# First compression layer of the samples: three products of 256 columns for each pair of neighbouring spans, chunks turned by 64-wide products

## The chip, the cores and the metric

One core of a Trainium2 chip runs the kernel. The metric is the device time of one execution in microseconds, the median of several.

## The reference

Two layers of a hybrid decoder trunk serve a prompt (512 rows) and a sample group (8 sequences of 4 new rows, with 1024 cached rows each) in one step. The case is about one function of it, the compression of keys and of values for sparse attention:

```python
def _compress(k, pos_emb, w1, w2):          # CMP_STRIDE = 16, hidden 256, 4 KV groups, HEAD_DIM 64
    ch = k[:, :n_chunk * 16].reshape(B, n_chunk, 16, N_KV, HEAD_DIM)
    first  = einsum('bcsgd,sdh->bcgh', ch + pos_emb[:16], w1[:16])
    second = einsum('bcsgd,sdh->bcgh', ch + pos_emb[16:], w1[16:])
    hid = silu(first[:, :-1] + second[:, 1:])
    return einsum('bngh,hd->bngd', hid, w2)
```

A span is two neighbouring chunks of 16 rows. Its hidden values are A c(n) + B c(n+1), with A the first half of w1, B the second and c(n) chunk n. A sample has 64 chunks and so 63 spans for each of 4 groups. The position term is the same for all spans and comes in as a bias. Everything else (projections, short convolution, attention, merge) is untouched.

## The kernel before

TensorE multiplies float32 in three passes: each operand is split into a high part (rounded, written by ScalarE, `...H`) and a low part (the rest, by VectorE, `...L`), and high x high, high x low and low x high are added up in PSUM. These products are of a type that the trace counts as one instruction. Plain float32 products show as two.

A layer runs: projections in feature order (line 769), projections in token order (line 940, six blocks, two buffers), compression, attention of the prompt with that of the samples between (64 units), and output projections.

**Compression** is ten units n = 0 to 9: n = 0 prompt keys, 1 to 4 keys of two samples each, 5 prompt values, 6 to 9 values of two samples each. A unit has four steps j, one for a quarter of the 16 rows of a chunk (rows 4q + j; two source rows, t = 0 and 1, stacked over 128 partitions). The orders of work on PE, ScalarE (act) and VectorE (dve) are written out by hand, one list for each engine, and joined by semaphores:

- `chunk_tp(n, j)` (line 967): PE turns the rows of `craw` for the step, 8 transposes of 128x128 into one of three PSUM banks in rotation. It stands in the middle of a step two ahead (`chunks_ahead`).
- `chunks_high` (ScalarE, line 1647) and `chunks_low` (VectorE, line 2128): eight instructions each of 64x256, from PSUM to `chH` and `chL`, which have two buffers (j % 2).
- `first_layer(n, j)`, line 1017: 24 products a step (2 halves of the hidden values x 4 quarters x 3 passes) of 504 columns, that is 2 samples x 63 spans x 4 groups. The quarters give both the A and the B part, since the moving operand starts `quarter` chunk halves later. For prompts (line 1012), H and L of the chunks go together, 264 and 132 columns.
- `hidden_gate` (ScalarE, line 1658, two sigmoids), `hidden` (VectorE, line 2149), `second_layer` (PE, lines 1035 and 1042), `compressed_out` (VectorE). `second_layer(n - 1)` follows step (n, 0).
- `beside` and `before_chunks`: parts of the prompt's compressed attention and key turns, put between the steps.
- Weights: one DMA from SP brings w1 of the keys (2 MB) into `w1_raw` during the token-order projections, one more brings that of the values as soon as the keys' parts are made. `w1_high` and `w1_low` (lines 1615 and 2100) split a quarter of it, 128x1024.
- After unit 9, PE does `scores(0)`, waits for `compressed_out(8)`, does `scores(1)` and then `second_layer(9)`.

Of the kernel before, what the change touches and what calls it, by code (L numbers as in the profile page):

```python
# [14 lines left out]
ds = bass.ds  # L15
# [130 lines left out]
def build(nc, a):  # L146
    ctx = ExitStack()
    with ctx:
# [96 lines left out]
        chH = at("chH", [P, 2, 2, P, GROUPS], W2, F32R)  # L245
        chL = at("chL", [P, 2, 2, P, GROUPS], W1, F32R)
# [3 lines left out]
        w1_raw = home("w1_raw", [P, 16, HID], M0)  # L250
        craw = [home("craw0", [P, 2, HC, KV], F0), at("craw1", [P, 2, HC, KV], H_H)]
        hidT = at("hidT", [P, 2, 504], 67072)
        hsg = at("hsg", [P, 2, 504], 71104)
        w2 = home("w2", [P, 2, 2, HD], M0 + 16384)
        kcp = [at("kcp0", [P, 2, SEQ], 128512), at("kcp1", [P, 2, SEQ], 76160)]
# [4 lines left out]
        cx = at("cx", [P, 2, SEQ], 80256)  # L260
# [79 lines left out]
        pos_ready = sem("pos_ready")  # L340
# [6 lines left out]
        c_sg, c_hid, c_w2, c_out = sem("c_sg"), sem("c_hid", 2), sem("c_w2", 1), sem("c_out", 1)  # L347
# [113 lines left out]
        def hidden_bank(n):  # L461

            return 4 + 2 * ((n + 1) % 2)
# [28 lines left out]
        def _(sp):  # L492
# [55 lines left out]
            def load_pages(l, n):  # L548

                slot, kv = sample_unit(n) % 2, n // 5  # L550
                numbers = page_numbers(n % 5 - 1)
                if n > 2:
                    sp.wait_ge(c_tp, 64 * l + 8 * sample_unit(n) - 8)
# [5 lines left out]
            def load_w1(l, name):  # L559

                sp.dma_start(w1_raw[:], a[name][ds(l, 1)].rearrange("l (k s) d h -> (s d) (l k) h", s=2)).then_inc(w1_in, 16)
# [9 lines left out]
            for l in range(NL):  # L571
# [14 lines left out]
                for i, c0 in enumerate(KV_COLS):  # L586
# [4 lines left out]
                    if i == 4:  # L591
                        sp.wait_ge(m_out, 16 * l + 16)
                        load_w1(l, "cmp_w1_k")
# [19 lines left out]
                sp.wait_ge(w1_lo, 8 * l + 4)  # L613
                load_w1(l, "cmp_w1_v")
# [4 lines left out]
                sp.wait_ge(c_tp, 64 * l + 64)  # L619
                sp.wait_ge(w1_lo, 8 * l + 8)  # L620
# [60 lines left out]
        def _(pool):  # L681
# [10 lines left out]
            for l in range(NL):  # L692
# [33 lines left out]
                pool.drain().then_inc(sa_q, 1)  # L726

# [21 lines left out]
        def _(pe):  # L749
# [80 lines left out]
            for l in range(NL):  # L830
# [123 lines left out]
                def chunk_tp(n, j):  # L954

                    slot = sample_unit(n) % 2
                    if j == 0:
                        pe.wait_ge(c_in[slot], 1024 * l + 256 * (sample_unit(n) // 2 + 1))
                    for s in range(2):
                        e = 8 * sample_unit(n) + 2 * j + s  # L960
                        if e < 3:
                            pe.wait_ge(tm_ev, nth(tm_ev, l * (5 * TM_BLOCKS) + 5 * TM_BLOCKS - 2))
                        else:
                            pe.wait_ge(c_lo, 64 * l + e - 2)
                        for k in range(4):
                            t, g2 = k // 2, k % 2
                            last = nc.tensor.transpose(ps[:, (e + 2) % 3, k * P:(k + 1) * P],  # L967
                                                       craw[slot][:, s, 2 * j + t, g2 * P:(g2 + 1) * P], ident)
                        last.then_inc(c_tp, 1)

                def chunks_ahead(n, j):

                    if n == 0 and j in (0, 3):
                        chunk_tp(1, int(j == 3))
                    elif n == 5 and j == 1:
                        chunk_tp(6, 1)
                    elif not prompt_unit(n) and j < 2:
                        chunk_tp(n, j + 2)
                    elif not prompt_unit(n) and n < 9 and (n, j) != (4, 3):
                        chunk_tp(n + 2 if n == 4 else n + 1, j - 2)  # L980

                def first_layer(n, j):


                    unit = 10 * l + n
                    nseq, nwin = windows(n)
                    if prompt_unit(n):
                        pe.wait_ge(kp_lo, 8 * l + 4 * (n // 5) + j + 1)
                        pe.wait_ge(w1_lo, 8 * l + (4 * (n // 5) + j + 1))
                    else:  # L990
                        pe.wait_ge(c_lo, 64 * l + 8 * sample_unit(n) + 2 * j + 2)
                    if j == 0:
                        pe.wait_ge(c_hid, nth(c_hid, 2 * unit - 2))
# [10 lines left out]
                    for hid in range(2):  # L1004
                        if hid == 1:
                            chunks_ahead(n, j)
                        for quarter in range(4):
                            span = slice(quarter, quarter + 2 * nwin - 1, 2)
                            if prompt_unit(n):
                                both, cols = pc_x[n // 5][j][:, :, span, :], nwin * GROUPS  # L1010
                                for w, x, width in ((w1H, both, 2 * cols), (w1L, both[:, 0], cols)):
                                    last = nc.tensor.matmul(ps[:, hidden_bank(n) + hid, 0:width], w[j][:, quarter, hid * P:(hid + 1) * P], x,
                                                            start=j == 0 and quarter == 0 and w is w1H, stop=j == 3 and quarter == 3 and w is w1L)
                                continue
# [1626 lines left out]
```

## Time and profile before

| what | value |
|---|---|
| median of 3 runs | 2436.61 us (2434.99 to 2437.31) |
| the profiled execution, its own time | 2438.41 us |
| its span | 2436.6 us, granted clock 0.991 on average |
| busy share PE / PE weight load / VectorE / ScalarE / GpSimd | 96 / 84 / 51 / 41 / 9% |
| compression, layer 1 | about 546 to 811 us |
| compression, layer 2 | about 1753 to 2018 us |

In a row of a view, "PE" is a matmul and "PEld" its weight load, L967 is line 967, `ps<-chH,w1H` means that `ps` is written from `chH` (moving) and `w1H` (stationary), `128*64 128x512` is a stationary tile of 128x64 with 512 moving columns. Durations of matmuls overlap, so their cost is read from start to start. In the chain that ended last, a piece's length is already its contribution to the end.

### The profile page before, as it was taken

The page shows a single profiled execution, that of the slowest core. Times are in us where ns is not written, and L with a number is a line of the kernel's source. Part 1 is how long each engine was busy: PE and PEld are TensorE (multiplying, and loading weights), DVE is VectorE, ACT ScalarE, POOL GpSimd, SP SyncE. Part 2 cuts the span into 40 slices and gives each one's busy share as a digit, 9 for nine tenths or more (in the row PEclk, how much of TensorE's full clock was granted, in tenths as well). Part 3 has the DMA queues.
Part 4 walks back from the last instruction along what each step waited for, and adds up shares of the span by engine and source line. Part 5 has one row for each costly group of instructions (what it writes and reads, how often), then busy time and mean ns, then how long its engine had stood idle before and what let it go on. Part 6 is the DMA issues. An engine that isn't in the chain of part 4 may idle for free.

```text
span 2436.6 us, 45477 instructions
## 1 busy us (share of the span) xinstructions
PE 2349.7 (96%) x17919; PEld 2052.9 (84%) x17919; DVE 1231.4 (51%) x2332; ACT 988.7 (41%) x2024; POOL 209.5 (9%) x349
## 2 busy tenths in 40 slices
PE   8999999999999999899989999999999999998998
PEld 8999999997778655589989999999977885555998
DVE  4444232546675566564454432234667655665544
ACT  4232223435564455533333221234446445554332
POOL 0000000000000233310000000000000002333000
PEclk9999999999999999999999999999999999999999
DMA  6343354707632687663234334546086418867530
GB/s 237 121 139 104 87 169 124 162 19 159 89 51 36 109 123 116 126 197 114 95 116 139 121 104 105 161 115 162 9 174 82 55 16 138 120 108 165 165 113 37
DMA packets 293308, 279.09 MB, mean 115 GB/s; under 512 B 92601, under 2 KB 281465, under 8 KB 291816
## 3 DMA queue, kind: packets, MB, share of 16 engines
q1 hardware_dynamic: 288680, 239.34, 45.1%
q0 software_dynamic: 4416, 36.85, 4.1%
q8 instruction: 142, 2.33, 0.4%
q14 instruction: 70, 0.57, 0.1%
HBM read 249.25 MB, written 43.53 MB: 120 GB/s over the span
## 4 chain that ended last, share of the span: by engine, by line
PE 86%; DVE 6%; ACT 3%; DMA 1%; issue 1%; SPq 1%; DVEq 0%; POOL 0%; ACTq 0%
PE ps L769 47%; PE ps L1017 12%; PE ps L940 7%; PE ps L1144 3%; PE ps L1168 3%; PE ps L1127 2%; DVE chL L2128 2%; PE ps L967 2%; PE ps L1266 2%; PE ps L1042 1%; ACT chH L1647 1%; PE ps L1414 1%; PE ps L1274 1%; SPq L567 1%; DMA v_win<-in_state_win 1%
## 5 line engine op out<-in xcount | busy, mean ns | idle before, releaser
L769 PE MATMUL ps<-hH,wH 128*128 128x272 f32 x2016 | 418.2, 289 | 8.5 <-DVE hL L1971 8.5
L403 DVE TENSOR_TENSOR wL<-w_raw,wH 128x2048 fp32r<-128x2048 f32 (+1 forms) x107 | 246.1, 2300 | 346.1 <-ACT wH L394 343.8
L769 PE MATMUL ps<-hH,wL 128*128 128x272 f32 x2016 | 420.1, 290 | 0.0
L769 PE MATMUL ps<-hL,wH 128*128 128x272 f32 x2016 | 416.9, 288 | 0.0
L769 PEld LDWEIGHTS ps<-hH,wH 128*128 128x128 f32 x2016 | 318.4, 189 | 10.3 <-issue 7.5
L769 PEld LDWEIGHTS ps<-hH,wL 128*128 128x128 f32 x2016 | 317.0, 189 | 0.0
L769 PEld LDWEIGHTS ps<-hL,wH 128*128 128x128 f32 x2016 | 316.9, 189 | 0.0
L2128 DVE TENSOR_TENSOR chL<-ps,chH 64x256 fp32r<-64x256 f32 x512 | 216.6, 423 | 152.6 <-ACT chH L1647 144.9
L1647 ACT ACTIVATE chH<-ps 64x256 fp32r<-64x256 f32 x512 | 207.4, 405 | 207.7 <-PE ps L1017 201.1
L394 ACT ACTIVATE wH<-w_raw 128x2048 fp32r<-128x2048 f32 (+1 forms) x107 | 204.9, 1915 | 97.6 <-PE ps L769 77.6
L739 POOL TENSOR_SCALAR pr<-pr,inv,zg 128x512 f32<-128x512 f32 (+3 forms) x256 | 154.0, 612 | 964.0 <-DVE inv L2323 964.0
L1017 PE MATMUL ps<-chH,w1H 128*128 128x504 f32 x512 | 208.9, 408 | 0.4 <-DVE chL L2128 0.4
L1017 PE MATMUL ps<-chH,w1L 128*128 128x504 f32 x512 | 200.4, 391 | 0.0
L1017 PE MATMUL ps<-chL,w1H 128*128 128x504 f32 x512 | 199.7, 390 | 0.0
L940 PE MATMUL ps<-wH,hH 128*128 128x264 f32 (+1 forms) x480 | 137.1, 286 | 0.0
L940 PE MATMUL ps<-wL,hH 128*128 128x264 f32 (+1 forms) x480 | 136.6, 285 | 0.0
L940 PE MATMUL ps<-wH,hL 128*128 128x264 f32 (+1 forms) x480 | 136.2, 284 | 0.0
L1757 ACT ACTIVATE pr<-ps,nmx 128x512 f32<-128x512 f32 (+3 forms) x256 | 132.2, 526 | 6.4 <-DVE nmx L2315 4.8
L2315 DVE TENSOR_REDUCE nmx<-ps 128x2 f32<-128x1024 f32 (+3 forms) x128 | 105.1, 823 | 36.8 <-PE ps L1132 34.7
L1144 PEld LDWEIGHTS ps<-con,pr 128*128 128x128 f32 x640 | 67.7, 141 | 65.5 <-POOL pr L739 47.8
L1168 PE MATMUL ps<-prT,zv 128*64 128x512 f32 (+3 forms) x512 | 97.2, 454 | 22.5 <-DVE prT L2329 19.6
L1017 PEld LDWEIGHTS ps<-chH,w1H 128*128 128x128 f32 x512 | 96.3, 188 | 26.5 <-issue 8.5
(337 smaller groups left out, 3972.9 us busy)
## 6 DMA issues: line engine op xcount, KB each, us to landing
w_raw<-in_w_in SPq DMA_DIRECT2D x59, 1024.0 KB
craw<-in_cache_kv SPq DMA_DIRECT2D x256, 128.0 KB, 5.0
w_raw<-in_w_in SPq DMA_DIRECT2D x64, 256.0 KB
k_sel<-in_cache_kv SPq DMA_DIRECT2D x128, 128.0 KB, 5.3
v_sel<-in_cache_kv SPq DMA_DIRECT2D x128, 128.0 KB, 10.3
out_new_win_sample<-in_state_win POOLq DMA_DIRECT2D x16, 1016.0 KB, 6.4
w_raw<-in_w_out_a SPq DMA_DIRECT2D x8, 1024.0 KB
k_win<-in_state_win SPq DMA_DIRECT2D x16, 512.0 KB, 7.3
```

Source lines behind the costliest of these rows:

```text
L394: act.activation(block_part(wH, b), block_part(w_raw, b), ACT.Copy).then_inc(w_hi, 1)
L403: dve.tensor_tensor(block_part(wL, b), block_part(w_raw, b), block_part(wH, b).bitcast(F32), ALU.subtract).then_inc(w_lo, 1)
L739: last = pool.tensor_scalar(pr[i % 3][:, g, 0:n], pr[i % 3][:, g, 0:n], inv[:, i % 3, g:g + 1], zg[:, u, gate:gate + 1], ALU.mult, ALU.mult)
L769: last = nc.tensor.matmul(ps[:, bank + hf, 0:HALF], st, x[:, k, hf * HALF:(hf + 1) * HALF], start=k == 0 and w is wH and x is xH, stop=k = ...
L940: last = nc.tensor.matmul(ps[0:rows, tt, 0:width], x[:, k, tt * P:tt * P + rows], w[:, n, k, 0:width], start=k == 0 and w is wH and x is h ...
L1017: last = nc.tensor.matmul(ps[:, hidden_bank(n) + hid, 0:nseq * nwin * GROUPS], w[j][:, quarter, hid * P:(hid + 1) * P], x, start=j == 0 an ...
L1144: last = nc.tensor.transpose(ps[:, 4 + g, kt * P:(kt + 1) * P], pr[i % 3][:, g, kt * P:(kt + 1) * P], ident)
L1168: last = nc.tensor.matmul(ps[rows, bank, kt * P:], zv[:, kt, v0:v0 + HD], turned_queries(g, br, kt), start=False, stop=i % 8 == 7)
L1647: last = act.activation(chH[64 * t:64 * t + 64, j % 2, s, :, g:GROUPS:2], src, ACT.Copy)
L1757: last = act.activation(pr[i % 3][:, g, 0:n], ps[:, 2 * (i % 2) + g, 0:n], ACT.Exp, bias=nmx[:, i % 3, g:g + 1], accum_out=sums[:, i % 3, ...
L2128: last = dve.tensor_tensor(chL[to], src, chH[to].bitcast(F32), ALU.subtract)
L2315: dve.tensor_reduce(out=nmx[:, i % 3, :], in_=ps[:, b:b + 2, 0:P * (unit(i)[2] + 1)], op=ALU.max, axis=AX.X, negate=True).then_inc(pa_nm, 1)
```

## The change

For two neighbouring spans the sums are formed from three products. With chunks 2k and 2k+1: P = A c(2k+1), Q = B c(2k), R = (A + B)(c(2k) + c(2k+1)). Then span 2k is R - P - Q, and span 2k+1 is P(k) + Q(k+1). Each has 256 columns (2 samples x 32 pairs x 4 groups).

- `first_layer`: 24 products of 256 columns (P and Q), then `chunk_tp` for a step two ahead, then 12 products of 256 columns (R) into a bank of its own (`joint_bank`).
- `chunk_tp`: 16 plain float32 products of a 64-wide stationary slice of `craw` with the identity, in pairs for the two halves of the output partitions, instead of 8 transposes. Both samples of a step land in banks 0 and 1, which have no second buffer: it waits for `chunks_low` of the step before.
- Splitting: `odd_chunks` (ScalarE, 128x512), `chunk_sum` (VectorE, 128x512), `chunks_high` (ScalarE, one of 128x1024), `chunks_low` (VectorE, one of 128x1024), `joint_high` (ScalarE, 128x512), `joint_low` (VectorE, 128x512).
- After a unit: `second_part` (ScalarE, 128x512), `hidden_sums` (VectorE, three dependent instructions of 496, 512 and 512 columns with drains), then gate and `hidden` as before. `second_layer(n - 1)` follows step (n, 1).
- Weights: `w1_sum` (VectorE), `w1_joint_high` (ScalarE) and `w1_joint_low` (VectorE), 128x512 each, eight of each in a layer. The joint keys' weights lie in `w1_raw` itself, so the values' weights come in four DMAs of 512 KB from GpSimd's queue, each after step (4, j) and after the DMA before it.
- `hidT` holds the spans of two samples interleaved, so the stationary operand of the values' second layer has a step of 8 elements, not 4.
- VectorE's `beside(4, 0)` and `beside(5, 1)`, with the multiplication of `cs` that stood at (6, 1), move behind `joint_low(7, 0)`, ahead of `chunk_sum(7, 1)`.

```diff
@@ chunk_tp
+                    if e:
+                        pe.wait_ge(c_lo, 96 * l + 3 * e - 1)
                     for s in range(2):
-                        for k in range(4):
-                            last = nc.tensor.transpose(ps[:, (e + 2) % 3, k * P:(k + 1) * P],
-                                                       craw[slot][:, s, 2 * j + t, g2 * P:(g2 + 1) * P], ident)
+                        for g in range(GROUPS):
+                            for t in range(2):
+                                last = nc.tensor.matmul(ps[HD * t:HD * t + HD, s, g * P:(g + 1) * P],
+                                                        craw[slot][:, s, 2 * j + t, g * HD:(g + 1) * HD], ident, start=True, stop=True)
+                    last.then_inc(c_tp, 1)
@@ first_layer, samples
+                    pe.wait_ge(c_lo, t + 2)
                     for hid in range(2):
+                        for odd in (1, 0):
+                            for q in range(2):
+                                ...
+                                for k, (w, x) in enumerate(((wH1, xH), (wH1, xL), (wL1, xH))):
+                                    nc.tensor.matmul(ps[:, bank, (0 if odd else 256):(256 if odd else 512)], w, x, ...)
+                    ...
+                        chunk_tp(n, j + 2)
+                    pe.wait_ge(c_lo, t + 3)
+                    for hid in range(2):
+                        for q in range(2):
+                            for k, (w, x) in enumerate(((SH, xH), (SH, xL), (SL, xH))):
+                                last = nc.tensor.matmul(ps[:, joint_bank(n), 256 * hid:256 * hid + 256], w[:, q, cols], x, ...)
+                    last.then_inc(c_mm, 1)
@@ act
+                def odd_chunks(n, j):
+                    act.wait_ge(c_tp, 32 * l + e + 1)
+                    act.wait_ge(c_lo, 96 * l + 3 * e)
+                    act.activation(ch_sum[:], turned_chunks(slice(2, 4)), ACT.Copy).then_inc(c_hi, 1)
@@ pool
+                for j in range(4):
+                    if l + j:
+                        pool.wait_ge(w1v_in, 64 * l + 16 * j)
+                    pool.wait_ge(c_mm, nth(c_mm, 40 * l + 17 + j))
+                    pool.dma_start(w1_raw[:, j:16:4, :], w1v[:, j:16:4, :]).then_inc(w1v_in, 16)
@@ dve, a unit boundary
+                    chunks_low(n, 1)
+                    hidden_sums(n - 1)
+                    joint_low(n, 1)
+                    chunk_sum(n, 2)
+                    hidden(n - 1)
+                    chunks_low(n, 2)
+                    joint_low(n, 2)
+                    chunk_parts(n, 3)
+                    compressed_out(n - 1)
+                    beside(n, 1)
```

## Rows read from the trace of the kernel before

**Rows 1.** The page, part 4: the chain that ended last, by line.
```profile
PE ps L769 47%; PE ps L1017 12%; PE ps L940 7%; PE ps L1144 3%; PE ps L1168 3%; PE ps L1127 2%; DVE chL L2128 2%; PE ps L967 2%; PE ps L1266 2%; PE ps L1042 1%; ACT chH L1647 1%; PE ps L1414 1%; PE ps L1274 1%; SPq L567 1%; DMA v_win<-in_st
```

**Rows 2.** Windows: stretch, width, busy time (x instructions), granted clock, DMA share, GB/s.
```profile
622.60:651.70 29.10, 28.12 (x133) 21.68 (x133) 18.33 (x40) 17.45 (x36) 0.00 (x0) 1.00 0.71 93
661.00:689.00 28.00, 24.80 (x147) 20.75 (x146) 24.01 (x50) 22.80 (x51) 0.00 (x0) 1.00 0.57 76
```

**Rows 3.** Chain that ended last, 540 to 740 us: start, us, what.
```profile
625.33 1.83 PE ps L1035 x4
627.17 2.94 PE ps L1017 x12
630.11 0.87 PE ps L967 x8
630.98 2.76 PE ps L1017 x12
...
637.89 2.76 PE ps L1017 x12
```

**Rows 4.** Timeline of PE, 43 rows of L940 in sequence, first and last.
```profile
535.82 0.29 PE L940 MATMUL ps<-wH,hH 128*128 128x264 f32 x1
...
540.96 0.29 PE L940 MATMUL ps<-wH,hH 128*128 128x264 f32 x1
```

**Rows 5.** Timeline of PE at 820 and at 870 us: start, duration.
```profile
820.40 0.44 PE L1168 MATMUL ps<-prT,zv 128*64 128x128 f32 x4
820.77 0.44 PE L1144 MATMUL ps<-con,pr 128*128 128x128 f32 x2
...
870.18 1.08 PE L1168 MATMUL ps<-prT,zv 128*64 128x512 f32 x4
871.19 1.09 PE L1144 MATMUL ps<-con,pr 128*128 128x128 f32 x8
```

**Rows 6.** Groups by form, whole span: busy us, mean ns | idle before.
```profile
L1647 ACT ACTIVATE chH<-ps 64x256 fp32r<-64x256 f32 x512 | 207.4, 405 | 207.7 <-PE ps L1017 201.1 <-PE ps L967 0.5
...
L1795 ACT ACTIVATE skT<-ps 128x512 f32<-128x512 f32 x64 | 37.2, 600 | 50.0 <-PE ps L1274 33.4 <-PE ps L1266 15.9
...
L1042 PEld LDWEIGHTS ps<-w,hidT 128*63 128x63 f32 x256 | 30.5, 212 | 2.6 <-DVE hidT L2149 2.6
...
L1168 PEld LDWEIGHTS ps<-prT,zv 128*64 128x64 f32 x512 | 27.5, 134 | 50.7 <-issue 27.2 <-ACT prT L1765 17.4
...
L2149 DVE SCALAR_TENSOR_TENSOR hidT<-ps,hb,hsg 128x504 f32<-128x504 f32 x32 | 22.3, 738 | 14.2 <-ACT hsg L1658 13.8
...
L2100 DVE TENSOR_TENSOR w1L<-w_raw,w1H 128x1024 fp32r<-128x1024 f32 x16 | 19.4, 1221 | 17.6 <-ACT w1H L1615 17.6
...
L1615 ACT ACTIVATE w1H<-w_raw 128x1024 fp32r<-128x1024 f32 x16 | 16.6, 1047 | 0.3
...
L2436 DVE TENSOR_TENSOR ssel<-ps,small 128x512 f32<-128x512 f32 x16 | 11.0, 686 | 16.2 <-PE ps L1274 16.2
```

**Rows 7.** Groups by form, 550 to 745 us.
```profile
L2234 DVE TENSOR_REDUCE cmx<-cs 128x64 f32<-128x2048 f32 x1 | 2.3, 2285 | 0.1
```

**Rows 8.** What PE waited for: us in total, times, longest.
```profile
PE ps L967 <- DVE chL L2128: 5.9, 18, 0.3
PE ps L1035 <- DVE hidT L2149: 5.4, 2, 2.7
```

**Rows 9.** Timeline of DVE, 528 to 596 us.
```profile
548.05 1.22 DVE L2100 TENSOR_TENSOR w1L<-w_raw,w1H 128x1024 fp32r<-128x1024 f32 x1 [7.64 <-ACT w1H L1615]
```

**Rows 10.** DMA issues: KB each, median us to landing.
```profile
pin<-in_p_prompt POOLq DMA_DIRECT2D x2, 512.0 KB, 4.2
```

**Rows 11.** Chain that ended last, 735 to 830 us.
```profile
795.52 13.79 PE ps L1017 x60
809.34 0.69 ACT hsg L1658
...
811.57 3.95 PE ps L1042 x32
```

More of the change, by code:

```diff
@@ L1004, in first_layer @@
                     for hid in range(2):
[L1005 to L1014, printed above, removed]
-                            xH, xL = (t[:, j % 2, :, span, :] for t in (chH, chL))
-                            for w, x, first, last_pass in ((w1H, xH, True, False), (w1H, xL, False, False), (w1L, xH, False, True)):
-                                last = nc.tensor.matmul(ps[:, hidden_bank(n) + hid, 0:nseq * nwin * GROUPS],
-                                                        w[j][:, quarter, hid * P:(hid + 1) * P], x,
-                                                        start=j == 0 and quarter == 0 and first, stop=j == 3 and quarter == 3 and last_pass)
@@ new lines, in first_layer @@
+                    SH, SL = w1_joint(n // 5, j)
+                    for hid in range(2):
+                        cols = slice(hid * P, hid * P + P)
+                        for q in range(2):
+                            xH, xL = chS[j % 2][:, 0, q], chS[j % 2][:, 1, q]
+                            for k, (w, x) in enumerate(((SH, xH), (SH, xL), (SL, xH))):
+                                last = nc.tensor.matmul(ps[:, joint_bank(n), 256 * hid:256 * hid + 256], w[:, q, cols], x,
+                                                        start=j + q + k + hid == 0, stop=j == 3 and q == 1 and k == 2 and hid == 1)
@@ new lines, in joint_low, with chunk_parts @@
+                def joint_low(n, j):
+                    e = place(n, j)
+                    dve.wait_ge(c_hi, 96 * l + 3 * e + 3)
+                    high, low = (chS[j % 2][:, k].rearrange("p q (k a) -> p q k a", k=32) for k in range(2))
+                    dve.tensor_tensor(low, ch_sum[:], high.bitcast(F32), ALU.subtract).then_inc(c_lo, 1)
+                def chunk_parts(n, j):
+                    chunk_sum(n, j)
+                    chunks_low(n, j)
+                    joint_low(n, j)
@@ L2280, in _ @@
                 w1_low(1, 0)
+                prompts_low(5, 1)
+                chunk_parts(6, 0)
                 w1_low(1, 1)
[L2282 to L2283 removed]
+                prompts_low(5, 2)
+                prompts_low(5, 3)
                 w1_low(1, 2)
+                hidden_sums(4)
+                w1_low(1, 3)
                 hidden(4)
[L2286 to L2288 removed]
+                chunk_sum(6, 1)
@@ L2289, in _ @@
                 chunks_low(6, 1)
-                compressed_out(4)
-                beside(5, 1)
-                hidden(5)
-                for n in (6, 7, 8):
+                hidden_sums(5)
+                joint_low(6, 1)
+                hidden(5)
+                w1_sum(1, 0)
+                w1_joint_low(1, 0)
+                compressed_out(4)
+                w1_sum(1, 1)
+                w1_sum(1, 2)
+                w1_joint_low(1, 1)
+                w1_sum(1, 3)
+                chunk_sum(6, 2)
@@ new lines, in _ @@
+                w1_joint_low(1, 2)
+                w1_joint_low(1, 3)
+                compressed_out(5)
+                chunks_low(6, 2)
+                joint_low(6, 2)
+                chunk_parts(6, 3)
+                beside(6, 1)
+                chunk_sum(7, 0)
+                before_chunks(6)
+                chunks_low(7, 0)
+                joint_low(7, 0)
+                beside(4, 0)
+                beside(5, 1)
+                chunk_sum(7, 1)
+                for n in (7, 8, 9):
+                    chunks_low(n, 1)
+                    hidden_sums(n - 1)
+                    joint_low(n, 1)
+                    chunk_sum(n, 2)
+                    hidden(n - 1)
@@ L2305, in _ @@
+                hidden_sums(9)
                 hidden(9)
```

425 lines of the change are left out of this document (279 added, 146 removed).

## The prediction

> **What bounds the kernel now.** I read the chain that ended last first: it is TensorE (PE) nearly throughout, and the line of the changed products, L1017, holds 12% of the span, the turning of chunks, L967, 2%, `chunks_low` 2% [rows 1]. So PE's time in the compression counts one to one. The windows show the same inside: in a stretch of the key units PE is busy 28.1 of 29.1 us, VectorE 18.3, ScalarE 17.5, at full clock. Only where the values start (661 to 689) does VectorE, with 24.0 of 28.0 us, hold PE up [rows 2]. In the chain of a unit the reader sees what a step costs: 2.76 (12 products) + 0.87 (8 transposes) + 2.76 = 6.39 us [rows 3]. The waits on PE say how often it lost time: 18 times `chunk_tp` waited for `chunks_low`, and twice the second layer for `hidden` [rows 8]. Where that happened a step took 637.89 - 630.98 = 6.91 us, 0.52 more than 6.39 [rows 3].
>
> **Products.** From start to start a product of 504 columns takes 13.79 / 60 = 0.2298 us [rows 11], one of 264 columns (540.96 - 535.82) / 42 = 0.1224 [rows 4]. The slope is 0.447 ns a column, so 256 columns cost 0.1188. A step has 24 x 0.2298 = 5.52 us before and 36 x 0.1188 = 4.28 after: 1.24 less, 64 steps (2 layers x 8 units x 4): **-79.3 us**. Bounds for one of 256: 0.1146, if the slope alone counts, and 0.1224, that of 264; I take the line through both.
>
> The Trainium skill, "TensorE: Matmul & The Clock Gate" (Back-to-back issue gap), gives N/2.4 + 2.5 ns, 109 ns for 256 columns; by it the sum would be 22 us lower. By that rule 264 columns would take 112.5 ns, and the trace has 122.4, so it does not agree.
>
> **Turning the chunks.** Before: 0.87 us [rows 3]. After: 8 pairs of plain float32 products, 64 wide, 128 columns. Exactly such pairs stand in the attention: with 512 columns a pair takes 871.19 - 870.18 = 1.01 us, with 128 columns 820.77 - 820.40 = 0.37 [rows 5]. The slope is 1.67 ns a column for both products together, 0.213 us a pair; what is left of 0.37, 0.157, is paid once on coming in. On going out, the first 12 products after such a block take 2.94, not 2.76: 0.18 [rows 3]. So 8 x 0.213 + 0.157 + 0.18 = 2.04 us, 1.17 more than before: **+74.9 us**. Bounds: 1.71, if neither end is paid, and from the weight loads. 32 loads and products of the values' second layer take 3.95 us, 0.123 each, paced by loads of 212 ns; the loads here take 134 [rows 6, 11]. Less the difference of 78 ns that is 0.045 an instruction, 1.45 us a block, no bound; in proportion it is 0.078, 2.49 us. I take the slope, since it is of the same form.
>
> The big gain of the products is thus given back by the turning, nearly to the last microsecond; the rest are waits.
>
> **Round trip of the turned chunks.** The two banks have no second buffer, so `chunk_tp` two ahead waits until `chunks_low` one ahead is done. From the end of one block to the start of the next PE has R (12 x 0.119 = 1.43), 0.18, P and Q (2.85): 4.46 us. In that time must run: end of PE to ScalarE 0.20 (a product lasts 0.17 beyond its slot [rows 4], then 809.31 to 809.34 [rows 11]), `odd_chunks` 0.60, `chunk_sum` 0.69, `chunks_high` 1.05, `chunks_low` 1.22 [rows 6], hand-overs about 0.2: 3.98. Slack 0.48 in a plain step, so the 18 waits of before go: 18 x 0.52 = **-9.4 us**. The 512-byte step of these reads I price at nothing, since L1647 reads so already at 405 ns for 256 columns [rows 6]; on the line between 600 for 512 and 1047 for 1024 that is within 30 ns. ScalarE and VectorE are relieved in total (8 x 0.41 against 2.25 us a step, 8 x 0.42 against 2.6), which is worth nothing by itself off the path.
>
> At a unit's boundary it does not fit. From the end of `chunks_low(n, 1)` there stand in a row: `hidden_sums` 3 x 0.69 + 0.2, `joint_low` 0.69, `odd_chunks` 0.60, two gates 1.38 [rows 11], `chunks_high` 1.05, `chunks_low` 1.22, hand-overs 0.25: 7.46. Counted from the start of unit n, `chunks_low(n, 1)` ends at 3.98 - 1.61 = 2.37, so `chunks_low(n, 2)` ends at 9.83. PE arrives for it after 2.85 + 1.86 + 0.18 + 1.43 + 2.85 = 9.17: wait 0.66, in units 2, 3, 4, 7, 8, 9 of both layers: **+7.9 us**.
>
> **Start of the keys.** `w1_sum` of the first two quarters lies in VectorE's idle 7.64 us [rows 9]; without it each would add 0.69. The others do not hide. Behind `chunks_low(1, 1)` VectorE has `hidden(0)` 0.6, `joint_low` 0.69, four weight instructions 2.76 (with 0.8 waiting for ScalarE's), `compressed_out(0)` 0.5 (the small ones are estimates, scaled down from 0.69 for 512 columns [rows 6]), and then 0.69 + 1.05 + 1.22 for the chunks of (1, 2): 8.3, that is 12.3 after the end of `chunk_tp(1, 1)`. PE gets there after 0.18 + 2.85 + 1.43 + 1.86 + 0.58 + 2.85 = 9.8: wait 2.5, and 0.3 ahead of unit 1. **+5.6 us** in two layers.
>
> **Start of the values.** The last quarter of w1 leaves only after step (4, 3): landing about 4.2 us (512 KB on this queue [rows 10]), 1.05, 1.22, with `hidden_sums(4)` of 2.3 in the way: 9.4 us after unit 4, where PE is ready after 7.8: wait 1.6 (0 to 2.8). From there VectorE has 11 instructions of 512 columns (7.6), two of 1024 (2.4), two hidden layers and two outputs (6.9), 17.5 with waits, before `chunks_low(6, 2)`; PE has 14.4 of work up to `chunk_tp(6, 3)`: wait 3.1 (0 to 4.9). Before, PE lost 2.7 + 0.5 here [rows 8]. **+3.0 us**. Then `beside(4, 0)` and `(5, 1)` stand ahead of `chunk_sum(7, 1)`: two instructions over 2048 columns at 2.29 [rows 7] and seven small ones, 1.5 by estimate, 6.1 us. `chunk_sum(7, 1)` ends 12.1 us after `chunk_tp(7, 0)`, `chunks_low(7, 1)` at 14.5, PE comes at 11.65: wait 2.8, **+5.6 us**. In the old places they hid beside PE's work.
>
> **The end.** Behind unit 9 nothing hides but two `scores`. Before: 811.57 - 809.31 = 2.26 us to `second_layer(9)` [rows 11]. After: 0.20 + 0.60 + 2.27 + 0.69 + 0.74 + 0.74 + 0.1 = 5.34. The attention's first gate and maxima stand behind it: **+6.2 us**.
>
> **Second layer of the values.** The stationary operand's step grows from 16 to 32 bytes. A load of 63 columns with step 16 takes 212 ns, one of 64 without a step 134 [rows 6], so a step costs. If it grows with the distance, eight blocks of 3.95 us double, +31 us; if it is only for leaving the neighbour, nothing. I take nothing, as nearer to a fixed price for each jump.
> The Trainium skill, "SBUF — State Buffer" (the note on cachelines), has lines of 16 bytes and a penalty for each new line; by that both steps pay alike, the sum is the same, and no run here has shown the step of 32 yet.
>
> **Sum.** -79.3 + 74.9 - 9.4 + 7.9 + 5.6 + 3.0 + 5.6 + 6.2 = +14.5 us, on the profiled execution's 2438.4, which stands 1.8 above the median. On the median: **2451 us**. About 5 us (0.2%) can be told from no change.
>
> **Rivals.**
> - *The narrow blocks cost no entry or exit* (the faster side). 64 x 0.34 = 21.7 less, 2429. It decides once a block costs under 2.04 - 14.5 / 64 = 1.81 us. For it: loads can run ahead inside a block. Against: both ends are in the rows [rows 3, 5]. 0.17.
> - *The products run at the slope alone*, 0.1146: 2304 x 0.0042 = 9.7 less, 2441. The row at 264 speaks against it. 0.06. By the gap rule of "TensorE: Matmul & The Clock Gate" in the Trainium skill it would be 22 less, 2429.
> - *Weight loads pace the narrow products.* Midway between 1.71 and 2.49, 0.39 x 64 = 25 more, 2476. 0.12.
> - *Round trip longer than PE's window*: strided reads or hand-overs 25% dearer make it 4.9, 0.4 of wait in some 50 steps, 2471. 0.12.
> - *Second layer of the values doubles*: 2482. 0.05.
> - *The two 64-wide products do not run side by side*: 1.71 x 64 = 109 more, 2560. The slope over 384 columns speaks against it. 0.03.
> - *The waits at starts and boundaries are half of mine* (the DMA lands early, queues overlap better): 28 becomes 14, 2437, no change that can be told. 0.12.
> - *The forecast*, 2443 to 2460: 0.33.
>
> Faster: 0.17 and half of the second, 0.20. Same: 0.15, the halved waits and the rest of the second. Slower: 0.65. The range has to reach 2430 below and 2477 above; the forecast's own is 2443 to 2460.
>
> **What would show it.** Right: 36 starts of L1017's successor at 0.119 us; `chunk_tp` from its first product to R's first in 2.0 us; PE waiting for `chunks_low` about 0.7 us once a unit, and 2 to 3 us in (1, 1), (6, 1) and (7, 0); 5.3 us from unit 9 to its second layer. Wrong: a block under 1.8 or over 2.3 us, a wait in every step, values' loads above 212 ns, or products away from 0.119.

## The result, and the profile after

The changed kernel takes **2459.9 us** (median of 4 runs, 2455.3 to 2463.1) against 2436.0 (2435.0 to 2437.3) for the kernel before in the same session: ratio 1.0096, 95% interval [1.0079, 1.0114], 24 us slower. The forecast was slower, 2451, with a range of 2430 to 2477. So the sign held, the size was 9 us short, and the parts came out less well than the total, as the part on the prediction shows. The profiled execution took 2463.1 us around a span of 2461.3, that is 24.7 above the span of the one before.

The page, part 1 (busy time, share, instructions), part 4 (the chain by line) and part 5 (costliest groups) of the changed kernel:

```profile
PE 2352.6 (96%) x20223; PEld 2109.5 (86%) x20223; DVE 1221.2 (50%) x2068; ACT 934.5 (38%) x1740; POOL 215.6 (9%) x357
...
PE 81%; DVE 8%; ACT 4%; DMA 3%; SPq 2%; issue 2%; DVEq 1%; POOL 0%; ACTq 0%; POOLq 0%
PE ps L812 46%; PE ps L983 7%; PE ps L1009 4%; PE ps L1064 4%; PE ps L1083 3%; PE ps L1232 2%; PE ps L1208 2%; PE ps L1191 2%; PE ps L1329 2%; DVE chL L2280 2%; PE ps L1106 1%; SPq L605 1%; ACT chH L1722 1%; DMA w_raw<-in_cmp_w_v 1%; PE ps 
...
L1009 PE MATMUL ps<-con,craw 128*64 128x128 f32 x2048 | 130.2, 282 | 17.4 <-DVE chL L2280 16.4
```

The 12% of the chain that the changed products held [rows 1] are now 4% (L1064, the products of even and of odd chunks) and 3% (L1083, those of the added ones). The turning of chunks (L1009) has gone from 2% to 4%, and a DMA of first-layer weights, which was not in that list before, has 1%.

What PE waited for (us in total, times, longest), against [rows 8]:

```profile
PE ps L1009 <- DVE chL L2280: 16.4, 10, 2.6
PE ps L1030 <- DVE w1L L2240: 10.3, 6, 2.6
...
PE ps L1106 <- DVE hidT L2321: 5.8, 2, 2.9
```

The 18 short waits of before (at most 0.3 us) are gone, as forecast. In their place stand 10 waits for the turned chunks, eight of them 1.5 to 2.6 us long, and 6 for weights of the values (L1030 are the prompt's products, which need them first).

The chain that ended last, in a plain step of the keys, against [rows 3]:

```profile
611.85 1.61 PE ps L1083 x12
613.46 0.87 PE ps L1123 x8
614.33 2.86 PE ps L1064 x24
617.20 1.90 PE ps L1009 x32
```

24 products in 2.86 us are 0.119 each, to the digit of the forecast. The block of 16 narrow products (x32, as each float32 product is two instructions) takes 1.90, and the 12 products behind it 1.61, where 12 without a block ahead take 1.39 (below, at the end): coming out of the block costs 0.22. A step is 2.86 + 1.90 + 1.61 = 6.37 us against 6.39. **The arithmetic that the change saves is worth next to nothing on this engine's path (0.02 us a step, about 1 us in 64); the 24 us are waits and what follows from them.**

To see where, I took the start of each unit's first product in both traces and subtracted. Sums over both layers; the forecast's terms are laid onto the same stretches (two of a unit's four chunk blocks run ahead of its first product, so unit 1 has two more and unit 9 two fewer than four):

| stretch | forecast, us | measured, us |
|---|---|---|
| up to the start of unit 2 | +8.6 | +4.6 |
| units 2 and 3 | -0.8 | -3.8 |
| start of unit 4 to start of unit 6 (the values' weights) | -2.6 | **+10.6** |
| unit 6 | +3.5 | +6.9 |
| unit 7 | +5.2 | +6.9 |
| unit 8 | -0.4 | -2.1 |
| unit 9, and up to its second layer | +1.1 | +0.1 |
| sum | +14.6 | +23.1 |

The remaining 1.6 of 24.7 us lies outside. One stretch is off by 13 us, the start of the values. The chain there, in the second layer:

```profile
1889.17 9.53 DMA w_raw<-in_cmp_w_v
...
1898.98 4.22 DMA w_raw<-in_cmp_w_v
...
1903.23 1.07 ACT w1H L1681
...
1904.32 1.24 DVE w1L L2240
...
1905.69 3.71 PE ps L1030 x16
1909.39 3.57 PE ps L1102 x4
```

The last quarter of the weights lands in 4.22 us, exactly the price taken from [rows 10], but the quarter ahead of it takes over 9.53, and GpSimd issues one only when the other has landed. In the first layer its timeline reads:

```profile
672.65 0.75 POOL L769 DMA_DIRECT2D w_raw<-in_cmp_w_v  x1 [8.43 <-PE ps L1083]
683.40 0.75 POOL L769 DMA_DIRECT2D w_raw<-in_cmp_w_v  x1 [10.01 <-DMA w_raw<-in_cmp_w_v]
```

Between the issues of the third and the last quarter 10.7 us pass. In that time SyncE's 16 page loads of unit 7, issued between 661.43 and 674.15, are on their way too. So the last step of unit 5 begins 13.7 us after unit 4 instead of 9.4.

The last two lines of the chain above show a second thing: four products of L1102 take 3.57 us, and 1.83 in a key unit. Windows of that stretch (busy times, then granted clock, DMA share, GB/s):

```profile
1899.00:1903.00 4.00, 2.31 (x20) 2.18 (x19) 3.29 (x6) 1.26 (x2) 0.73 (x1) 0.98 0.47 131
1903.00:1913.00 10.00, 7.75 (x24) 4.65 (x23) 4.51 (x6) 3.77 (x5) 0.00 (x0) 0.50 0.00 0
1913.00:1917.00 4.00, 4.00 (x42) 3.87 (x44) 2.55 (x7) 2.20 (x5) 0.00 (x0) 0.99 0.00 0
```

PE had stood idle for 1.69 us up to 1901.18 and for 2.25 up to 1905.69, and from 1903 to 1913 its clock was granted at 0.50, which is 1.2 instead of 2.4 GHz. The same follows three of the four waits for turned chunks of over 1.8 us. Timeline and windows of unit (7, 0), first layer, and two rows of unit 6, the first from the first layer, the second from the same place in the second:

```profile
726.98 2.29 DVE L2419 TENSOR_TENSOR cs<-cs,cgw 128x2048 f32<-128x2048 f32 x1
729.18 0.68 DVE L2274 TENSOR_TENSOR ch_sum<-ps,ch_sum 128x512 f32<-128x512 f32 x1
...
731.02 1.22 DVE L2280 TENSOR_TENSOR chL<-ps,chH 128x1024 fp32r<-128x1024 f32 x1 [1.15 <-ACT chH L1722]
...
732.30 3.52 PE L1009 MATMUL ps<-con,craw 128*64 128x128 f32 x32 [2.61 <-DVE chL L2280]
...
708.84 1.97 PE L1009 MATMUL ps<-con,craw 128*64 128x128 f32 x32 [1.86 <-DVE chL L2280]
1926.23 3.21 PE L1009 MATMUL ps<-con,craw 128*64 128x128 f32 x32 [1.86 <-DVE chL L2280]
```

```profile
729.00:732.00 3.00, 0.69 (x6) 0.49 (x5) 1.85 (x3) 2.03 (x3) 0.00 (x0) 1.00 0.00 0
732.00:735.00 3.00, 2.70 (x26) 2.71 (x28) 2.73 (x5) 0.00 (x0) 0.00 (x0) 0.52 0.00 0
735.00:738.00 3.00, 3.00 (x29) 2.83 (x26) 1.66 (x4) 2.13 (x4) 0.00 (x0) 0.91 0.00 0
```

The queue is the forecast one: `beside(4, 0)` and `(5, 1)` stand ahead of `chunk_sum(7, 1)` (L2274), and PE waits 2.61 us (forecast 2.8). But the block then takes 3.52 instead of 1.97, at a clock of 0.52: wait and slow block cost 4.2 us. The two rows of unit 6 separate the one from the other: behind the same wait of 1.86 us the clock fell in the second layer and stayed in the first, and unit 6 takes 32.8 us there and 31.2 here. So this low clock cost 1.6 us beside the wait, and a wait of this length doesn't always bring it. Over the two compression stretches:

```profile
540.00:840.00 300.00, 280.32 (x2783) 253.08 (x2781) 171.94 (x264) 124.33 (x215) 9.07 (x13) 0.98 0.50 80
1750.00:2060.00 310.00, 291.70 (x2844) 262.92 (x2842) 178.53 (x275) 130.84 (x237) 9.84 (x14) 0.97 0.51 78
```

300 x 0.02 + 310 x 0.03 = 15.3 us of full clock are missing; added up in pieces of 5 us it is the same 15.3, and in the kernel before 1.8. Not all of it is lost time: behind the last wait of each layer, 2.9 us ahead of unit 9's second layer, the clock is low too, and the 32 products there take 4.05 us (below) where they took 3.95 [rows 11]. These two stretches hold 3.4 of the 15.3. Of the other 12 some 10 are lost, by an estimate that takes 1.6 us for each of the four single stretches and the 1.7 us each by which L1102 and the L1030 products ahead of it are slow in the one at 1903. No term of the forecast held this. The Trainium skill, "TensorE: Matmul & The Clock Gate" (What's actually happening), has the throttled state as the default, released by activity, with two levels and nothing between. The rows agree as to the levels (0.50 and 1.00; the others are windows that hold some of each) and as to which side an idle engine falls.

The end of the stage, against [rows 11]:

```profile
816.57 1.39 PE ps L1083 x12
...
822.27 0.74 DVE hidT L2321
823.06 4.05 PE ps L1106 x32
```

From the last product, 817.96, to the second layer it is 5.1 us (forecast 5.34, before 2.26).

### The profile page after: what moved, and what is told of

Its sections match the earlier page's. It is cut to its first block, busy times and chain, and to the rows that moved or that the text cites. A ratio compares the mean times of both kernels' runs of the same rounds, so it can differ in the third digit from the quotient of the medians.

```text
span 2461.3 us, 49690 instructions
## 1 busy us (share of the span) xinstructions
PE 2352.6 (96%) x20223; PEld 2109.5 (86%) x20223; DVE 1221.2 (50%) x2068; ACT 934.5 (38%) x1740; POOL 215.6 (9%) x357
## 4 chain that ended last, share of the span: by engine, by line
PE 81%; DVE 8%; ACT 4%; DMA 3%; SPq 2%; issue 2%; DVEq 1%; POOL 0%; ACTq 0%; POOLq 0%
PE ps L812 46%; PE ps L983 7%; PE ps L1009 4%; PE ps L1064 4%; PE ps L1083 3%; PE ps L1232 2%; PE ps L1208 2%; PE ps L1191 2%; PE ps L1329 2%; DVE chL L2280 2%; PE ps L1106 1%; SPq L605 1%; ACT chH L1722 1%; DMA w_raw<-in_cmp_w_v 1%; PE ps L1477 1%
## 5 line engine op out<-in xcount | busy, mean ns | idle before, releaser
L1064 PE MATMUL ps<-chH,w1H 128*128 128x256 f32 x512 | 147.8, 289 | 0.0
L1009 PE MATMUL ps<-con,craw 128*64 128x128 f32 x2048 | 130.2, 282 | 17.4 <-DVE chL L2280 16.4
L1064 PE MATMUL ps<-chL,w1H 128*128 128x256 f32 x512 | 144.6, 282 | 0.0
L1064 PE MATMUL ps<-chH,w1L 128*128 128x256 f32 x512 | 144.5, 282 | 0.0
L1009 PEld LDWEIGHTS ps<-con,craw 128*64 128x64 f32 x2048 | 114.6, 140 | 27.0 <-DVE chL L2280 21.0
L1713 ACT ACTIVATE ch_sum<-ps 128x512 f32<-128x512 f32 x64 | 38.1, 596 | 194.6 <-PE ps L1009 161.8
## 6 DMA issues: line engine op xcount, KB each, us to landing
v_sel<-in_cache_kv SPq DMA_DIRECT2D x128, 128.0 KB, 10.5
```

What stands on the lines that cost most here:

```text
L1009: last = nc.tensor.matmul(ps[HD * t:HD * t + HD, s, g * P:(g + 1) * P], craw[slot][:, s, 2 * j + t, g * HD:(g + 1) * HD], ident, start=Tru ...
L1064: nc.tensor.matmul(ps[:, bank, (0 if odd else 256):(256 if odd else 512)], w, x, start=j + q + k == 0 and odd == 1, stop=j == 3 and q == 1 ...
```

## The experiments

Theories after the result. **A**: page loads beside the values' weights delay them; with the longer queue of VectorE ahead of `chunk_sum(7, 1)` and the clock behind each long wait they make up the excess. **B** (rival): the narrow blocks are dearer on the path than 1.90 us and the 0.2 on the way out (before_narrow speaks to this), or VectorE's total work is now the bound (split_beside, which moves work and removes none). The times of the kernel before differ a little between sessions (2435.7 to 2437.1), so the ratios are what is compared.

### wide8: full-width turning in the changed kernel

In place of 16 products 64 wide, 8 transposes 128 wide. The turned chunks then stand in another order, so that the kernel computes another function, at the same sizes.

```diff
-                        for g in range(GROUPS):
-                            for t in range(2):
-                                last = nc.tensor.matmul(ps[HD * t:HD * t + HD, s, g * P:(g + 1) * P],
-                                                        craw[slot][:, s, 2 * j + t, g * HD:(g + 1) * HD], ident, start=True, stop=True)
+                        for k in range(4):
+                            last = nc.tensor.transpose(ps[:, s, k * P:(k + 1) * P],
+                                                       craw[slot][:, s, 2 * j + k // 2, (k % 2) * P:(k % 2 + 1) * P], ident)
```

> The changed kernel, with the chunks turned by 8 wide transposes a step instead of 16 narrow products (the turned chunks then lie in another order, so the compressed samples' keys and values are other numbers; all else is the same work). Theory 1, the narrow block costs what it takes: 1.94 us and 0.22 on the way out against 0.87, so 64 x 1.25 = 80 us less, of which 5 to 15 come back as waits at the unit boundaries, since PE now arrives earlier: 2385 to 2395 us. Theory 2, PE would wait for the round trip of the turned chunks anyway and the block's length hides in it: 2420 us or more.

Measured: 2422.7 us (2420.0 to 2427.7), ratio 0.9948 [0.9932, 0.9965], 37 us less than the changed kernel. What PE waited for:

```profile
PE ps L1008 <- DVE chL L2279: 36.7, 22, 3.8
```

The time lies where theory 2 put it, 2420 or more, and 30 us above theory 1, which allowed for 5 to 15 us of new waits. But of the block's length not all hides: 64 x 1.23 = 79 us of PE's work left, and 37 came back as time. Waits for turned chunks went from 16.4 us to 36.7, and 20.4 us of clock are missing in the two stretches, not 15.3. The narrow blocks are on the path, but half of their extra length covers queues that would show without them. The 20 us of new waits for chunks and 5 us of clock do not make up all of the 42 that stayed; the rest is not accounted for.

### before_narrow: the narrow turning alone

The kernel before, with each transpose made as a pair of 64-wide products. Its output is that of the kernel before.

```diff
-                            last = nc.tensor.transpose(ps[:, (e + 2) % 3, k * P:(k + 1) * P],
-                                                       craw[slot][:, s, 2 * j + t, g2 * P:(g2 + 1) * P], ident)
+                            for h in range(2):
+                                c0 = g2 * P + h * HD
+                                last = nc.tensor.matmul(ps[HD * h:HD * h + HD, (e + 2) % 3, k * P:(k + 1) * P],
+                                                        craw[slot][:, s, 2 * j + t, c0:c0 + HD], ident, start=True, stop=True)
```

> The kernel before, with each of its transposes written as two narrow products for the two halves of the output partitions, nothing else changed. Theory 1: 64 x (2.1 - 0.87) = 75 to 80 us more, 2511 to 2516 us. Theory 2, the length of the block hides in waits: less than 2480 us.

Measured: 2496.0 us (2493.8 to 2496.3), ratio 1.0242 [1.0227, 1.0258], 60 us slower. Its chain, and its windows:

```profile
630.90 1.90 PE ps L969 x32
632.80 2.96 PE ps L1019 x12
635.76 1.83 PE ps L1037 x4
```

```profile
540.00:840.00 300.00, 298.81 (x2205) 239.70 (x2205) 165.37 (x369) 141.30 (x328) 0.00 (x0) 1.00 0.43 68
1750.00:2060.00 310.00, 308.86 (x2334) 252.75 (x2334) 178.59 (x407) 149.16 (x350) 0.00 (x0) 1.00 0.42 66
```

The same 1.90, and 2.96 instead of 2.76 [rows 3] for the 12 products behind it: the price of a block, 1.90 + 0.2 - 0.87 = 1.23 us, belongs to the narrow form and not to the new products. Both theories missed: theory 1 counted all blocks in full, theory 2 was 16 us too low. 64 x 1.23 less the 9.4 us of waits that go is 69; a further 5 are the waits of the second layer for `hidden`, 5.4 us before [rows 8] and 0.5 here. 60 were measured, and the last 4 us are not placed. And the clock is 1.00 throughout: narrow products alone don't bring it down. In this kernel no wait of PE in the two stretches reaches 1 us; in the changed kernel every low stretch there follows a wait of 1.7 us or more.

### hold_pages: the page loads of unit 7 behind the weights

SyncE waits for the values' weights before it issues the page loads of unit 7.

```diff
+                    if n == 7:
+                        sp.wait_ge(w1v_in, 64 * l + 64)
```

> The changed kernel, with the page loads of unit 7 held until the values' weights have landed. Theory 1, the third quarter of the weights took 10.5 us because 16 page loads of 128 KB ran beside it: it lands in 4 to 6 us, the last step of unit 5 starts 5 us earlier, 3 to 5 us a layer reach the end: 2450 to 2454 us. Theory 2, the load is slow by its own rows and queue: the landing stays at 10 us and the time at 2460.

Measured: 2452.3 us (2449.2 to 2454.7), ratio 1.0067 [1.0053, 1.0080], some 7 us less, as theory 1 had it. GpSimd's timeline:

```profile
672.65 0.75 POOL L771 DMA_DIRECT2D w_raw<-in_cmp_w_v  x1 [8.44 <-PE ps L1085]
677.07 0.75 POOL L771 DMA_DIRECT2D w_raw<-in_cmp_w_v  x1 [3.67 <-DMA w_raw<-in_cmp_w_v]
```

4.4 us between the two issues instead of 10.7. From unit 4 to unit 6 it is 43.1 us in both layers, where the changed kernel has 47.2 and 48.1: 9 us of the 13 that the forecast lacked there. The waits for weights shrink from 2.6 to at most 1.4 us, and no low clock follows them. So the 9 hold both the waits and the slow products behind them. The cause of this part is shown; 4 of the 13 us stay, and hold_swap takes up 3 of them.

### beside_back: the two beside works at an earlier place

`beside(4, 0)` and `beside(5, 1)` on VectorE go from ahead of `chunk_sum(7, 1)` to between `prompts_low(5, 3)` and `w1_low(1, 2)`.

```diff
+                beside(4, 0)
+                beside(5, 1)
                 w1_low(1, 2)
...
-                beside(4, 0)
-                beside(5, 1)
                 chunk_sum(7, 1)
```

> The changed kernel, with the two pieces of compressed attention that stood ahead of the chunk sum of (7, 1) moved into the wait of VectorE for the values' weights. Theory 1: the wait of 2.6 us in step (7, 0) and the slow block behind it (3.5 us at a granted clock of 0.69) go: 3.5 to 4.5 us a layer, 2451 to 2453 us. Theory 2, VectorE is the bound of this stretch, so the work costs the same wherever it stands: 2460.

Measured: 2463.5 us (2459.4 to 2465.1), ratio 1.0106 [1.0090, 1.0121]: nothing gained. The wait at (7, 0) is gone, and this has come:

```profile
PE ps L1030 <- DVE w1L L2240: 15.5, 4, 7.1
```

The number is nearer to theory 2 (2460) than to theory 1 (2451 to 2453). In that place VectorE is what makes the weights ready; the 6 us stood in another queue that was just as full. That the wait was caused by these two works was not refuted, only this place for them; split_beside tries another.

### hold_swap, hold_pool, hold_all: VectorE's queue

On top of hold_pages. hold_swap takes the next chunks ahead of the second layer at unit boundaries:

```diff
                     joint_low(n, 1)
+                    hidden_sums(n - 1)
                     chunk_sum(n, 2)
...
                     joint_low(n, 2)
+                    hidden(n - 1)
```

(moved down from ahead of `joint_low(n, 1)` and of `chunks_low(n, 2)`; ScalarE's list likewise). hold_pool makes the eight sums of weights a layer on GpSimd:

```diff
+                def w1_sum(kv, j):
+                    pool.wait_ge(w1_lo, w1_dve(l, "low", kv, j))
+                    pool.tensor_tensor(w1_raw[:, j:8:4, :], w1_raw[:, j:8:4, :], w1_raw[:, 8 + j:16:4, :], ALU.add).then_inc(sa_q, 1)
```

hold_all has both.

> The changed kernel with the page loads of unit 7 held until the values' weights have landed (hold_pages, 2452.3 us), and at six unit boundaries a layer the order of ScalarE and VectorE altered: the chunk sum and both chunk copies of the next unit's first span come ahead of the second layer and gate of the unit before. Theory 1: the 0.3 to 0.6 us that TensorE waits for the first turned chunks at a boundary are the queue behind that other work; 12 boundaries give 3 to 7 us, so 2445 to 2449 us, and the wait at the start of unit (7,0), 2.6 us, shrinks too. Theory 2: VectorE's sum of work in a unit sets these waits, and a new order only moves them to the next span: 2451 to 2454 us. If the second layer now comes later for its consumer, over 2455 us.

> The changed kernel with the page loads held as in hold_pages (2452.3 us), and the eight sums of first-layer weights a layer (0.69 us each on VectorE) made by GpSimd. Theory 1: at the start of the values and of the keys VectorE is the last to finish what TensorE waits for; with 4 x 0.69 us out of its queue at the values and 2 at the keys, up to 4 us a layer come back: 2444 to 2449 us. Theory 2: GpSimd's sum takes longer than VectorE's (a 128 x 512 operation of it took 1.26 us) and stands itself in the path of the joint products: 2451 to 2458 us.

> Both edits (the boundary order and the sums on GpSimd) on top of the held page loads. If each waits for its own queue they add: 2438 to 2444 us, ratio to the kernel before 1.001 to 1.003. If both only relieve the same VectorE queue, no better than the better one of them: 2445 to 2450 us. If neither is on the path: 2452 us.

Measured, in one session:

| kernel | us | ratio |
|---|---|---|
| hold_swap | 2449.5 (2447.2 to 2451.2) | 1.0053 [1.0040, 1.0067] |
| hold_pool | 2451.5 (2450.1 to 2453.5) | 1.0062 [1.0049, 1.0076] |
| hold_all | 2449.1 (2446.2 to 2451.5) | 1.0049 [1.0035, 1.0063] |

The order at the boundaries gives about 3 us, at the edge of what was expected. The intervals of hold_swap and hold_pages overlap, but the traces show the gain and where it lies. At the boundaries of units 2, 3, 8 and 9 the waits were 0.3 us and not the forecast 0.66, and these units get 0.2 us shorter each. At that of unit 4 the changed kernel waits 1.55 us in each layer:

```profile
659.26 1.97 PE L1009 MATMUL ps<-con,craw 128*64 128x128 f32 x32 [1.55 <-DVE chL L2280]
```

This wait is gone in hold_swap, and the stretch from unit 4 to unit 6 goes from 43.1 to 41.5 us in both layers.

The wait at (7, 0), which theory 1 expected to shrink too, stayed at 2.61 us in the first layer.

The sums on GpSimd (1.3 us each: its busy time is 236.3 us with them and 215.6 in the changed kernel, for 16) give nothing that can be told, and the two edits do not add. PE's waits for chunks fall from 17.0 us in hold_pages to 10.9 in hold_pool, and unit 6 gets 2.5 us shorter in each layer, but the stretch ahead of it, from unit 4, gets 1.6 longer. VectorE's timeline shows one reason; the first row runs while GpSimd makes a sum from 678.55 on, the second alone:

```profile
678.35 2.57 DVE L2251 TENSOR_TENSOR w1L<-w_raw,w1H 128x1024 fp32r<-128x1024 f32 x1
685.00 1.22 DVE L2251 TENSOR_TENSOR w1L<-w_raw,w1H 128x1024 fp32r<-128x1024 f32 x1
```

The instruction, whose inputs both lie in SBUF, takes longer by about GpSimd's 1.3 us, and so do the 64x128 ones of `prompts_low` (up to 1.25 us for 0.38). The VectorE instructions of `hidden_sums`, which have an input in PSUM, are not slowed (0.69 us either way). So a sum taken off VectorE was in part paid back by VectorE waiting beside it. Theory 2 of hold_pool held in result. Of its reason the sum's length is in the trace (1.3 us against 0.69); what the trace adds is that VectorE's own instructions stand still beside it.

### wide8_all: what is left with short blocks

hold_all with the edit of wide8 (and again another order of the turned chunks).

> hold_all with the sixteen narrow products of a chunk block replaced by eight full-width ones (the turned chunks then stand in another order, so the kernel computes another function at the same sizes). wide8, without the three edits on the queues, took 2422.7 us and had 36.7 us of waits for turned chunks. Theory 1: those waits are order and landing, and the edits take half of them: 2400 to 2412 us. Theory 2: VectorE's sum of work binds once the block is short, and only the two sums a layer start and the held loads help: 2412 to 2419 us. The gap between this kernel and hold_all is then the price of the narrow products on the path: 64 x 0.9 = 58 us if nothing hides it, some 30 us if half of it is hidden.

Measured: 2401.4 us (2399.0 to 2404.4), ratio 0.9855 [0.9840, 0.9870]. Theory 1 held: 21 us less than wide8. The gap to hold_all is 48 us of the 79 of PE's work. Even so the edits leave waits in units that gain nothing. The chain in unit 2, keys:

```profile
600.66 0.56 SPq L595
601.40 5.47 DMA craw<-in_cache_kv
...
606.92 1.10 PE ps L1019 x8
```

The block of eight waits for a page load that SyncE issued at 600.66. In the first layer unit 2 takes 30.96 us there and 31.03 in the kernel before, while unit 8 takes 25.5 against 31.2 (in the second layer unit 2 takes 28.3). With PE's work gone, the issue and landing of pages limit this unit; PE's other waits for chunks still come to 13.4 us.

### split_beside: one of the two beside works a step earlier

hold_swap, with `beside(4, 0)` moved into an idle time of VectorE one step ahead.

```diff
                 beside(6, 1)
+                beside(4, 0)
                 chunk_sum(7, 0)
...
-                beside(4, 0)
                 beside(5, 1)
                 chunk_sum(7, 1)
```

> hold_swap (2449.5 us) with beside(4, 0), the sum of 2.28 us over the compressed scores and a small one, taken from between joint_low(7, 0) and beside(5, 1) on VectorE and put one step earlier, behind beside(6, 1), where VectorE was idle for 2.8 us in the trace of the changed kernel (715.9 to 718.7). Theory 1: the wait of 2.6 us ahead of the second chunk block of unit 7 is the queue of VectorE at just that place, and the block of 3.5 us instead of 1.97 is the lower granted clock behind that wait: both go, 2 x (2.5 + 1.5) = 8 us less, 2441 to 2444 us. Theory 2: the wait goes but the low clock has another cause and stays, as in beside_back: 5 us less, 2444 to 2447 us. Theory 3: VectorE as a whole is the bound of this stretch, so that the wait only moves one step ahead: 2448 to 2451 us.

Measured: 2444.6 us (2438.3 to 2447.9), ratio 1.0036 [1.0022, 1.0049], some 4 us less than hold_swap. Timeline and windows of the place where the changed kernel waited 2.61 us:

```profile
723.76 1.97 PE L1011 MATMUL ps<-con,craw 128*64 128x128 f32 x32 [0.16 <-DVE chL L2282]
```

```profile
729.00:732.00 3.00, 3.00 (x43) 2.73 (x41) 2.56 (x4) 1.11 (x2) 0.00 (x0) 1.00 0.03 5
732.00:735.00 3.00, 3.00 (x26) 2.84 (x24) 0.91 (x2) 1.87 (x3) 0.00 (x0) 1.00 0.22 69
```

The wait is 0.16, the block 1.97, and the clock 1.00. Unit 7 takes 31.5 us against 33.9 in hold_swap and 35.5 in the changed kernel (first layer). Over both layers it is 6.4 us less than in hold_swap, whose rows for this place are:

```profile
726.57 1.97 PE L1011 MATMUL ps<-con,craw 128*64 128x128 f32 x32 [2.61 <-DVE chL L2282]
1937.38 3.62 PE L1011 MATMUL ps<-con,craw 128*64 128x128 f32 x32 [2.25 <-DVE chL L2282]
```

There the longer wait had no slow block behind it and the shorter one had. So theory 1's 8 us took for granted a slow block in each layer, and in that trace only one was there to be saved. The median, 2444.6, lies just above theory 1's range, at the lower end of theory 2's; the profiled execution was the fastest of its five, so 4 us is the number to keep. The intervals of this ratio and of hold_swap's overlap, so it is the traces that carry the reading: the wait is gone and has not come back a step earlier. That speaks against theory 3, and against the half of B that made VectorE's total work the bound. This is the best of the versions that compute the reference, and it is still 9 us slower than the kernel before.

## Why the prediction was right, and where it was short

**Products, -79.3.** Right to the digit: 0.119 us each. The Trainium skill, "TensorE: Matmul & The Clock Gate" (Back-to-back issue gap), gives 109 ns for 256 columns by a formula for products by themselves, and the trace does not agree for these float32 products, each with its own weight load.

**Turning, +74.9.** Right in kind, 4 us small: 1.23 us a block and not 1.17. The rival without entry and exit is refuted by two kernels, with 0.2 us on the way out in each; the rival of 2.49 us, paced by loads, too.

**18 waits gone, -9.4; second layer of the values, 0.** Right. With the step of 32 bytes the 32 loads and products take 3.94 us from their start to that of the next product, where they took 3.88 in the kernel before; the 3.95 of [rows 11] runs to the end of the last one. That is 0.5 us in eight blocks, where doubling would have been 31. By the Trainium skill, "SBUF — State Buffer" (the note on cachelines), both steps pay for a new line alike; the trace agrees within these 0.06 us.

**Boundaries, +7.9, and key start, +5.6.** Too large but for one. These are the first rows of a boundary, keys, first layer:

```profile
599.22 0.28 PE L1064 MATMUL ps<-chH,w1L 128*128 128x256 f32 x1
599.62 1.97 PE L1009 MATMUL ps<-con,craw 128*64 128x128 f32 x32
```

The last product's slot ends at 599.34, so the wait is 0.28, not 0.66. Unit 4 is the exception, with 1.55 (hold_swap). At the key start the wait is 1.5 and not 2.5, but the one ahead of unit 1 is 0.9 and not 0.3. By the table the forecast was 4 us too high up to unit 2, of which the waits explain 1, and 3 us in units 2 and 3. There 1.5 us are the shorter waits; the rest is that 8 of the 18 waits of before stood in these two units, while the table spreads them evenly.

**Start of the values, +3.0.** This is the term that was mis-sized: it took the 4.2 us of one undisturbed transfer [rows 10], in a stretch in which, as [rows 2] show with a DMA share of 0.57, others were on the engines, and it let the last quarter leave right after step (4, 3), though by the change that quarter waits for the one before it. That one took 10.5. The stretch from unit 4 to unit 6 came out 13 us dearer than forecast; hold_pages gives 9 of them back in the traces (7 in the medians of the whole kernel) with two lines on SyncE, and the order of hold_swap 3 more.

**Late `chunk_sum(7, 1)`, +5.6.** Place, cause and length of the wait are right (2.61 against 2.8); what it set off was missing, 1.5 us of a slow block each. The same holds for the values' start and, in the second layer, for unit 6. So the general omission is one of kind: the forecast priced a wait at its own length, and took the clock of [rows 2], 1.00, for granted in a kernel with 14 waits of PE over 1 us in the two stretches, where the one it was read from has two.

**The end, +6.2.** Right, 0.2 us a layer too high: 5.1 against 2.26, in two layers 5.7.

By the table, the forecast was 10 us too high for the key start, the boundaries and the last two units, and 18 too low from the values' start to unit 7; 8 of the difference are left, +24 where +14.5 was forecast. So the total came closer than its parts, and that was luck: two errors of opposite sign. What stays open is why the clock fell behind some waits and not behind others of the same length, so that its share of the 24 us can be told for this trace (some 10, an estimate) but not foretold. It is not even the same from one execution to the next: of the changed kernel's four, the one with a mean granted clock of 0.991 took 2455.3 us and the one with 0.986, the profiled one, 2463.1.

## What to carry to other kernels

Fewer columns are worth only what the layout that they need leaves over: here 1.24 us a step were paid for with 1.23 us of half-width turning. Price a transfer in the company it will have, and ask whether its issue waits for the landing of another. A wait of TensorE can cost more than its length, by a slow stretch behind it (1.6 us here, not each time); to take it away, move work of the late engine into a gap one step ahead (split_beside, 4 us), not into another full queue (beside_back, nothing).

## What the runs showed of the hardware that was not expected

- Behind waits of 1.4 to 2.9 us, though not behind each of them (1.42, the shortest, in split_beside), the granted clock went to 0.50, and 3.21 to 3.62 us were paid for a block of 1.97. It was not the longer waits that did it: in one kernel (hold_swap) the clock stayed at 1.00 behind 2.61 us and fell behind 2.25. Once, after two such waits 4.5 us apart, it stayed at 0.50 for 10 us.
- A kernel whose only change was more work for TensorE (before_narrow), and whose waits shrank by it, kept a clock of 1.00 in the two compression stretches, where the kernel before lacks 1.8 us of it.
- A 512 KB transfer of the queue of GpSimd took 4.2 us alone and 10.5 beside sixteen page loads of 128 KB (9.5 in the second layer); with these loads held back, the same quarter took 4.2.
- While GpSimd added two 128x512 operands in SBUF (1.3 us), VectorE instructions with both inputs in SBUF took longer: 2.57 for 1.22 us, up to 1.25 for 0.38 (hold_pool). Those with an input in PSUM kept their 0.69.
- Of 79 us of TensorE work taken out (wide8), 37 came back as time, and 48 once the queues around it were rearranged.
